# The state-space stage of a hybrid layer: the skip term D x made and added by GpSimd, finished chunks turned two chunks later, rows of u loaded by SyncE

## The chip, the cores and the metric

The kernel runs on one core of one Trainium2 chip. The metric is the device time of one execution in microseconds; the median of three runs stands for a kernel.

## What is computed

One layer of a network that mixes attention and a two-way state-space scan (Mamba-2 SSD), for 1024 latent and 256 context tokens, in 32-bit floats. The change lies in the state-space part alone. Of the reference, cut to that part:

```python
CHUNK = 128            # 10 chunks of 128 tokens: 8 latent, 2 of context
SSM_HEADS, SSM_HEAD_DIM, D_STATE = 8, 64, 128

def ssd_chunked(x, dt, a, bm, cm, init_state):
    ...
    lmat = jnp.exp(jnp.where(causal, seg, -jnp.inf))            # seg: differences of cumulated dt * a
    cb = jnp.einsum("bclgn,bcsgn->bgcls", cc, bc)
    y_diag = jnp.einsum("bgcls,bgrcls,bcsgrp->bclgrp", cb, lmat, xr)
    ...
    final, entering = lax.scan(step, init_state, (chunk_decay, chunk_states))
    y_off = jnp.einsum("bclgn,cbgrpn,bgrcl->bclgrp", cc, entering, jnp.exp(a_cs))
    y = (y_diag + y_off).reshape(b, l, h, p)
    return y, final.reshape(b, h, p, n)

def ssm_mixer(...):
    ...
    y_f, fin_f = ssd_chunked(xs, dt_f, a_f, bm, cm, init_f)
    y_b, fin_b = ssd_chunked(flip(xs), flip(dt_b), a_b, flip(bm), flip(cm), init_b)
    y = y_f + flip(y_b) + d_skip.astype(f32)[:, None] * xs.astype(f32)
    y = y.reshape(b, l, SSM_WIDTH) * jax.nn.silu(z.astype(f32))
    return rms_norm(y, g_out).astype(z.dtype), fin_f, fin_b
```

## The kernel before

The kernel is written engine by engine: each engine has its own list of instructions in an order set by hand, and semaphores between them. A wait stands in front of an instruction, and everything behind it on that engine waits too. `phase_front` holds the input projection, the gate z, a backward sweep over the chunks that makes the backward states, and then the loop over the ten chunks (`for c in range(NT)`) that this case is about. Before the loop TensorE turns x, token by feature, chunk after chunk (`turn_x`), and ScalarE copies it out of PSUM into `xs(c)`, a part of `chunks_hi`; the untransposed x stays in `xbcT`.

For one chunk c of the loop, PSUM banks are called A[0] to A[3] and Q (four banks):

- **TensorE** makes the two carried products into A[1] and A[2] (line 1431), then the exponents' differences of the chunk after, `segments(c + 1)`, into Q: four times a product of `up` with `pick` (line 1391) and one that adds the mask (line 1393). Rows 64 and 65 of `pick` hold this chunk's rows of u, loaded from DRAM. Then `contribution(c)` to the state (line 1368), `scores(c + 1)` (line 1414), and into A[3] the skip term as four products with a diagonal matrix `ddiag` (line 1443) and the in-chunk product with the weights `wt` (line 1448). Last it turns the finished rows of the chunk before, `y_turn(c - 1)`, into A[0] (line 1399).
- **VectorE** scales A[1] and A[2] by the decays (lines 1158 and 1160, the second into `off_b`), adds the two (line 1164), makes the next state (line 1150) and the weights of the next chunk (lines 1137 and 1140), then adds A[3] (line 1171) and multiplies by the gate (line 1172), which is `y_ready`.
- **ScalarE** squares the finished y with a sum (`square`, line 864, into `yn`), takes the exponential of Q (`exponents`, line 875) and copies the scores to `cb` (line 877), scales y to `yn` (`scale`, line 869), copies the turned rows from PSUM over the gate (`mix`, line 881, which is `mix_ready`), and weighs x for the next contribution (`weigh`, line 888, eight instructions).
- **GpSimd** decays the forward state (line 685), makes the reciprocal root of the mean square (`rstd`, lines 690 and 691), and issues the load of u for chunk c + 2 (line 697).
- **SyncE** waits for `mix_ready`, stores the chunk's mixed rows (line 627), waits for that store and loads attention's rows over them (`load_landed`, lines 388 to 390).

Q, A[0] and A[3] are single. `pick`, `yv`, `wt`, `xw` and the state `sf` have two slots each. In the code P is 128, NT is 10, NT_LAT is 8, NS is 9, and SW is 512.

Of the kernel before, what the change touches and what calls it, by code (L numbers as in the profile page):

```python
# [23 lines left out]
P = 128  # L24
F32 = mybir.dt.float32
# [10 lines left out]
NT = T // P  # L36
# [35 lines left out]
C_GPRE, C_GFFN, C_BMOD, C_GQ, C_GKV, C_CW, C_CB, C_GS, C_DB, C_AL, C_DS = 0, 8, 16, 64, 67, 69, 93, 101, 105, 121, 137  # L72
N_COLS = 141
# [319 lines left out]
def phase_front(L):  # L393
# [6 lines left out]
    with ExitStack() as st:  # L400
# [31 lines left out]
        ddiag = at("ddiag", "conv_acc", 2048, [P, 4, P])  # L432
# [31 lines left out]
        def turn_bank(n):  # L464
# [17 lines left out]
        u_loaded = [L.own_sem(f"ss_u{i}") for i in range(2)]  # L482
# [6 lines left out]
         rstd_ready, yn_ready, y_turned, mix_ready, sf_ready, dec_ready, fin_mm, fin_cp, consts, pch) = (  # L489
# [4 lines left out]
                 "sf_ready", "dec_ready", "fin_mm", "fin_cp", "consts", "pch"))  # L494
# [48 lines left out]
        dskip = L.cols[:, C_DS:C_DS + 4]  # L543
# [20 lines left out]
        def _(sp):  # L564
# [51 lines left out]
            sp.wait_ge(q_stored, 16)  # L616
            for c in range(NT):
# [7 lines left out]
                if c < NT - 1:  # L625
                    sp.wait_ge(mix_ready, c + 1)
                    sp.dma_start(quads(L.mixS[c]), zt(c)).then_inc(mix_stored, 16)

        @block.gpsimd
        def _(pool):  # L630
# [45 lines left out]
            p.link(pool.memset(nh[:], -0.5))  # L676

# [15 lines left out]
            def load_u(c):  # L693

                if c >= 2:
                    pool.wait_ge(seg_done, c - 1)
                pool.dma_start(pick[64:66, c % 2, :, :], L.u_s[:, :, chunk(c)]).then_inc(u_loaded[c % 2], 16)

            until(pool, tiles[-1])
            load_u(0)  # L700
            load_u(1)
# [11 lines left out]
        def _(act):  # L713
# [119 lines left out]
            def constants(i):  # L833
# [26 lines left out]
            def square(c):  # L860
                act.wait_ge(y_ready, c + 1)
                if c >= 1:
                    act.wait_ge(y_turned, c)
                act.activation(yn[:], yv[:, c % 2, :], ACT.Square, accum_out=ss[:, c:c + 1]).then_inc(squared, 1)

            def scale(c):
                act.wait_ge(rstd_ready, c + 1)
                act.wait_ge(squared, c + 1)
                act.activation(yn[:], yv[:, c % 2, :], ACT.Copy, scale=rs[:, c:c + 1]).then_inc(yn_ready, 1)
# [2547 lines left out]
```

## Time and profile before

| | |
|---|---|
| median of three runs | 1667.59 us (1666.72 to 1667.93) |
| the profiled execution | 1670.06 us, its span 1668.2 us |
| TensorE busy / VectorE / ScalarE / GpSimd, share of the span | 97% / 61% / 42% / 6% |
| the loop over chunks | from about 350 to 428 us of the span |
| granted TensorE clock, whole span | 0.994 of full |

The profile is of one execution. "PE" is TensorE's matmul, "DVE" VectorE, "ACT" ScalarE, "POOL" GpSimd, "SPq" the issue of a DMA by SyncE. Starts of neighbours on one engine can lie closer than the duration printed, since the end of one overlaps the start of the next; the distance from start to start is then what an instruction costs.

### The profile page before, as it was taken

The numbers are of one execution on the slowest core, as the hardware profiler recorded it, in microseconds if no ns is written. First come the engines' busy times: TensorE is split into PE (matmuls) and PEld (weight loads), VectorE is DVE, ScalarE is ACT, GpSimd is POOL, SyncE is SP. The second block draws the span as 40 slices with busy tenths as digits, with TensorE's granted clock in tenths as the row PEclk, the third lists the DMA queues.
The fourth block names the chain that finished last, engine by engine and source line by source line (L and its number), as shares of the span: only waits on it lengthen the run. The fifth ranks groups of instructions, "written<-read, shape, count | busy, mean of one in ns | idle before, by whom it ended". The sixth has DMA issues, their size and how long they took to land. (4 is left out here: it accounts for less than half of the span.)

```text
span 1668.2 us, 25023 instructions
## 1 busy us (share of the span) xinstructions
PE 1621.0 (97%) x9735; PEld 1414.1 (85%) x9735; DVE 1017.8 (61%) x1689; ACT 705.7 (42%) x1288; POOL 100.4 (6%) x123
## 2 busy tenths in 40 slices
PE   6999999999899999999999999999999999999997
PEld 4787878877688988878889999999999998888886
DVE  4653645268655555554587656666665665477788
ACT  4632112357554444545664333333333334434453
POOL 1101000013000000320000000000000000000011
PEclk9999999999999999999999999999999999999999
DMA  9324441013200000323312222212222226663445
GB/s 372 149 98 145 158 155 52 1 56 105 74 20 1 14 1 1 108 89 133 127 51 87 97 80 93 106 73 98 91 97 81 92 81 219 232 217 97 126 162 191
DMA packets 76294, 176.36 MB, mean 106 GB/s; under 512 B 10353, under 2 KB 26945, under 8 KB 74129
## 3 DMA queue, kind: packets, MB, share of 16 engines
q1 hardware_dynamic: 72080, 169.75, 29.3%
q0 software_dynamic: 4096, 5.01, 0.9%
q8 instruction: 79, 1.29, 0.3%
q14 instruction: 39, 0.31, 0.1%
HBM read 131.02 MB, written 43.70 MB: 105 GB/s over the span
## 5 line engine op out<-in xcount | busy, mean ns | idle before, releaser
L374 PE MATMUL psF<-gv,gu_ring 128*128 128x384 f32 (+1 forms) x664 | 220.6, 332 | 3.9 <-DVE gv L2748 3.2
L375 PE MATMUL psF<-gv,gu_ring 128*128 128x384 f32 (+1 forms) x664 | 220.1, 332 | 0.0
L376 PE MATMUL psF<-gv,gu_ring 128*128 128x384 f32 (+1 forms) x664 | 220.1, 331 | 0.0
L381 PE MATMUL psF<-gv,gu_ring 128*128 128x512 f32 x540 | 193.6, 392 | 0.0
L382 PE MATMUL psF<-gv,gu_ring 128*128 128x256 f32 x540 | 151.3, 280 | 0.0
L374 PE MATMUL psF<-d_w_ring,d_hid_ring 128*128 128x512 f32 x360 | 140.2, 389 | 0.0
L375 PE MATMUL psF<-d_w_ring,d_hid_ring 128*128 128x512 f32 x360 | 140.1, 389 | 0.0
L376 PE MATMUL psF<-d_w_ring,d_hid_ring 128*128 128x512 f32 x360 | 140.1, 389 | 0.0
L374 PEld LDWEIGHTS psF<-gv,gu_ring 128*128 128x128 f32 x664 | 125.3, 189 | 10.4 <-issue 3.6
L375 PEld LDWEIGHTS psF<-gv,gu_ring 128*128 128x128 f32 x664 | 125.5, 189 | 0.0
L374 PE MATMUL psP<-hT_hi,win_hi 128*128 128x512 f32 (+1 forms) x336 | 123.7, 368 | 1.8 <-DVEq L1085 1.5
L376 PEld LDWEIGHTS psF<-gv,gu_ring 128*128 128x128 f32 x664 | 125.3, 189 | 0.0
L376 PE MATMUL psP<-hT_hi,win_lo 128*128 128x512 f32 (+1 forms) x336 | 119.2, 355 | 0.0
L375 PE MATMUL psP<-hT_lo,win_hi 128*128 128x512 f32 (+1 forms) x336 | 119.1, 354 | 0.0
L2543 ACT ACTIVATE hraw<-psF 128x384 f32<-128x384 f32 (+1 forms) x130 | 56.8, 439 | 138.9 <-PE psF L376 84.2
L381 PEld LDWEIGHTS psF<-gv,gu_ring 128*128 128x128 f32 x540 | 101.1, 187 | 16.6
L382 PEld LDWEIGHTS psF<-gv,gu_ring 128*128 128x128 f32 x540 | 101.9, 189 | 0.0
L1846 DVE TENSOR_TENSOR pt_lo<-psPT,pt_hi 128x512 fp32r<-128x512 f32 (+1 forms) x104 | 58.9, 583 | 43.8 <-ACT pt_hi L1706 43.6
L2590 ACT ACTIVATE d_hid_ring<-d_hid 128x640 fp32r<-128x640 f32 x54 | 40.0, 740 | 98.4 <-PE psF L376 98.4
L374 PEld LDWEIGHTS psF<-d_w_ring,d_hid_ring 128*128 128x128 f32 x360 | 67.6, 188 | 14.6 <-DVE hraw L3007 0.5
L375 PEld LDWEIGHTS psF<-d_w_ring,d_hid_ring 128*128 128x128 f32 x360 | 67.6, 188 | 14.0
L376 PEld LDWEIGHTS psF<-d_w_ring,d_hid_ring 128*128 128x128 f32 x360 | 67.6, 188 | 13.9
(457 smaller groups left out, 3704.3 us busy)
## 6 DMA issues: line engine op xcount, KB each, us to landing
hid_variants<-hraw SPq DMA_DIRECT2D x77, 320.0 KB, 2.2
d_hid<-hid_variants SPq DMA_DIRECT2D x58, 320.0 KB, 3.0
m_wring<-in_w_mod SPq DMA_DIRECT2D x16, 1024.0 KB, 4.9
d_b<-in_w_down SPq DMA_DIRECT2D x44, 256.0 KB, 4.5
win_raw<-in_w_in SPq DMA_DIRECT2D x18, 512.0 KB, 5.7
w_mod_staged<-in_w_mod SPq DMA_DIRECT2D x16, 512.0 KB, 15.3
d_hid_more<-hid_variants SPq DMA_DIRECT2D x19, 320.0 KB, 3.2
raw_gu<-in_w_gate SPq DMA_DIRECT2D x11, 512.0 KB, 3.8
```

The lines of the kernel that those rows point to most:

```text
L374: pe.matmul(out, w_hi, x_hi, start=first, stop=False, skip_group_check=onto)
L375: pe.matmul(out, w_hi, x_lo, start=False, stop=False, skip_group_check=onto)
L376: return pe.matmul(out, w_lo, x_hi, start=False, stop=last, skip_group_check=onto)
L381: pe.matmul(both, w_hi, x_both, start=first, stop=False, skip_group_check=onto)
L382: return pe.matmul(main, w_lo, x_hi, start=False, stop=last, skip_group_check=onto)
L1846: dve.tensor_tensor(pt_lo[:, g[0]:g[-1] + 1, r:r + P], psPT[:, (g0 + i) % 2, 0:len(g), :], pt_hi[:, g[0]:g[-1] + 1, r:r + P].bitcast(F32), ...
L2543: act.activation(dst[:, chunk(c)], psA(n, c), ACT.Copy).then_inc(main_copied if paired_up(n, c) else copied[c], 1)
L2590: act.activation(ring_h(e, 0), hr[e % HR], ACT.Copy).then_inc(h_hi, 1)
```

## The change

The skip term leaves TensorE. GpSimd makes `xd(c)`, x times D in token order, for all ten chunks before the loop, over the x in `xbcT` that has been turned. In the loop it adds xd(c) to `off_b` and then `off_b` to `yv` (`carried`), which VectorE did in one instruction before; VectorE waits for `y_summed` ahead of its addition of A[3]. `ddiag` and its 40 products go, and the four ScalarE instructions that filled it.

ScalarE's `weigh(c + 1)` now follows its exponentials directly, then comes `mix` of chunk c - 2 (it was c - 1), and `scale(c - 1)` last. TensorE's `y_turn` is of chunk c - 2 in pass c. The squares go to a tile of their own.

The rows of u of chunks 0 and 1 are loaded by GpSimd as before. The others are loaded by SyncE: chunks 2 and 3 ahead of its loop, chunk c + 4 at the end of its pass c.

```diff
+        sq_junk = at("y_sq_junk", "conv_acc", 2048, [P, SW])
+        dskip = at("d_skip", "conv_acc", 4608, [P, SH])[:]
...
+        xd = lambda c: L.xbcT[:, 0:4, chunk(c)]
@@ block.sync
+            def load_u(c):
+                sp.wait_ge(seg_done, c - 1)
+                sp.dma_start(pick[64:66, c % 2, :, :].bitcast(F32), L.u_s[:, :, chunk(c)]).then_inc(u_later[c % 2], 16)
+
+            load_u(2)
+            load_u(3)
             for c in range(NT):
                 if c >= 1:
                     sp.wait_ge(mix_stored, 16 * c)
                     load_landed(L, sp, in_hi, c - 1)
...
                 if c < NT - 1:
                     sp.wait_ge(mix_ready, c + 1)
                     sp.dma_start(quads(L.mixS[c]), zt(c)).then_inc(mix_stored, 16)
+                if c + 4 < NT:
+                    load_u(c + 4)
@@ block.gpsimd
+            pool.wait_ge(kr_stored, 32)
+            for i, c in enumerate(down):
+                pool.wait_ge(x_copied, 2 * i + 1)
+                p.mark(pool.tensor_tensor(heads4(xd(c)), heads4(xs(c)), per_head(dskip), ALU.mult))
+            p.wait()
+
+            def carried(c):
+
+                pool.wait_ge(off_b_read, c + 1)
+                p.link(pool.tensor_tensor(quads(off_b[:]), quads(off_b[:]), xd(c), ALU.add))
+                pool.wait_ge(off_f_read, c + 1)
+                pool.tensor_tensor(yv[:, c % 2, :], yv[:, c % 2, :], off_b[:], ALU.add).then_inc(y_summed, 1)
 
             pool.wait_ge(s_ready, NS)
             for c in range(NT):
                 decay(c)
+                carried(c)
                 if c >= 1:
                     rstd(c - 1)
-                if c + 2 < NT:
-                    load_u(c + 2)
@@ block.scalar
                     exponents(c + 1)
+                    weigh(c + 1)
+                if c >= 2:
+                    mix(c - 2)
                 if c >= 1:
                     scale(c - 1)
-                    mix(c - 1)
-                if c + 1 < NT:
-                    weigh(c + 1)
+            mix(NT - 2)
@@ block.vector
-                dve.wait_ge(off_f_read, c + 1)
-                dve.wait_ge(off_b_read, c + 1)
-                f.link(dve.tensor_tensor(yv[:, c % 2, :], yv[:, c % 2, :], off_b[:], ALU.add))
-
                 if c + 1 < NT:
                     next_state(c)
                     weights_in_chunk(c + 1)
 
+                dve.wait_ge(y_summed, c + 1)
                 dve.wait_ge(diag_done, c + 1)
@@ block.tensor
-                pe.wait_ge(u_loaded[c % 2], 16 * (c // 2 + 1))
+                if c < 2:
+                    pe.wait_ge(u_loaded[c], 16)
+                else:
+                    pe.wait_ge(u_later[c % 2], 16 * (c // 2))
...
-                for a in range(4):
-                    pe.matmul(A[3][:, chunk(a)], L.xbcT[:, a, chunk(c)], ddiag[:, a, :], start=(a == 0), stop=False)
...
-                if c >= 1:
-                    if c + 1 < NT:
-                        pe.wait_ge(cb_read, c + 2)
-                    if c >= 2:
-                        pe.wait_ge(mix_ready, c - 1)
-                    y_turn(c - 1)
+                if 2 <= c < NT - 1:
+                    pe.wait_ge(cb_read, c + 2)
+                    if c >= 3:
+                        pe.wait_ge(mix_ready, c - 2)
+                    y_turn(c - 2)
+            pe.wait_ge(mix_ready, NT - 2)
+            y_turn(NT - 2)
```

What stands on ScalarE in one pass of the loop, before. `seg` is the exponential, `cb` the copy of the scores, `yn<-yv,y_rs` the scaling, `chunks_hi<-psP` the mix, `xw` the weighing, and `yn,y_ss<-yv` the square:

```order
L875 ACTIVATE seg<-psP 128x2048 [waits ss_seg_done,ss_w_ready]
L877 ACTIVATE cb<-psP 128x256 [waits ss_cb_done]
L869 ACTIVATE yn<-yv,y_rs 128x512 [waits ss_squared,ss_rstd]
L881 ACTIVATE chunks_hi<-psP 128x4x128 [waits ss_y_turned]
L888 ACTIVATE xw<-chunks_hi,dt_feats 128x64 [waits ss_s_mm]
L888 ACTIVATE xw<-chunks_hi,dt_feats 128x64 x7
L864 ACTIVATE yn,y_ss<-yv 128x512 [waits ss_y_turned,ss_y_ready]
```

And now:

```order
L891 ACTIVATE seg<-psP 128x2048 [waits ss_seg_done,ss_w_ready]
L893 ACTIVATE cb<-psP 128x256 [waits ss_cb_done]
L904 ACTIVATE xw<-chunks_hi,dt_feats 128x64 [waits ss_s_mm]
L904 ACTIVATE xw<-chunks_hi,dt_feats 128x64 x7
L897 ACTIVATE chunks_hi<-psP 128x4x128 [waits ss_y_turned]
L885 ACTIVATE yn<-yv,y_rs 128x512 [waits ss_y_turned,ss_squared,ss_rstd]
L878 ACTIVATE y_sq_junk,y_ss<-yv 128x512 [waits ss_squared,ss_y_ready]
```

The weighing moved ahead of the mix and the scaling behind it; the exponential and the mix of one pass now have the eight weighing instructions between them.

What stands on SyncE in one pass of its loop, before (`ssm_mix_scratch` takes the mixed rows, the three loads behind it are attention's):

```order
L627 DMA ssm_mix_scratch<-chunks_hi 512x1x128 [waits ss_mix_ready]
L388 DMA chunks_hi<-q_scratch 128x3x128 [waits ss_mix_stored]
L389 DMA chunks_hi<-kv_scratch 128x2x128
L390 DMA chunks_hi<-kr_scratch 128x128
L627 DMA ssm_mix_scratch<-chunks_hi 512x1x128 [waits ss_mix_ready]
```

And now:

```order
L635 DMA ssm_mix_scratch<-chunks_hi 512x1x128 [waits ss_mix_ready]
L621 DMA pick<-u_scratch 2x16x128 [waits ss_seg_done]
L388 DMA chunks_hi<-q_scratch 128x3x128 [waits ss_mix_stored]
L389 DMA chunks_hi<-kv_scratch 128x2x128
L390 DMA chunks_hi<-kr_scratch 128x128
```

The load of u came between the store of a chunk and the wait for that store, so behind the wait for `mix_ready`.

What stands on TensorE now from one contribution to the next segments (`m_psC` is A[3], `m_psM` is A[2], `psP` holds Q, A[0] and A[1]):

```order
L1382 MATMUL psP<-xw,chunks_lo 128x256 [waits ss_xwf_ready,ss_off_f_read]
L1382 MATMUL psP<-xw,chunks_lo 128x256
L1431 MATMUL psP<-xbcT 128x128 [waits ss_mix_ready,ss_cb_read]
L1431 MATMUL psP<-xbcT 128x128
L1467 MATMUL m_psC<-chunks_hi,wt 32x64 [waits ss_w_ready,ss_y_ready]
L1467 MATMUL m_psC<-chunks_hi,wt 32x64 x31
L1416 MATMUL psP<-const,yn 128x128 [waits ss_yn_ready,ss_mix_ready,ss_cb_read]
L1416 MATMUL psP<-const,yn 128x128 x3
L1448 MATMUL psP<-sf,xbcT 128x256 [waits ss_off_b_read,ss_sf_ready]
L1448 MATMUL psP<-sf,xbcT 128x256
L1448 MATMUL m_psM<-chunks_lo,xbcT 128x256 x2
L1408 MATMUL psP<-pick,up_49 128x512 [waits ss_u_later1,ss_exp_done]
```

The four products with `ddiag` that stood ahead of the in-chunk product are gone, and the first product of the segments waits for SyncE's load instead of GpSimd's.

## Rows read from the trace of the kernel before

**Rows 1.** Timeline of TensorE, one pass: start us, us, engine, line, tiles

```profile
365.45 1.03 PE L1431 MATMUL psP<-sf,xbcT 128*128 128x256 f32 x4
...
367.00 0.58 PE L1391 MATMUL psP<-pick,up 66*128 66x512 f32 x1
...
369.02 1.03 PE L1368 MATMUL psP<-xw,chunks_lo 128*128 128x256 f32 x4
...
370.33 1.06 PE L1443 MATMUL m_psC<-ddiag,xbcT 128*128 128x128 f32 x8
371.32 1.10 PE L1448 MATMUL m_psC<-chunks_hi,wt 128*32 128x64 f32 x64
...
372.84 1.03 PE L1431 MATMUL psP<-sf,xbcT 128*128 128x256 f32 x4
```

**Rows 2.** Timeline of VectorE, the same pass; idle before it in brackets

```profile
368.13 0.68 DVE L1160 TENSOR_TENSOR off_b<-m_psM,dt_feats 128x512 f32<-128x512 f32 x1
368.92 0.70 DVE L1164 TENSOR_TENSOR yv<-yv,off_b 128x512 f32<-128x512 f32 x1
370.14 0.69 DVE L1150 TENSOR_TENSOR sf<-decayed,psP 128x512 f32<-128x512 f32 x1 [0.52 <-PE psP L1368]
371.19 1.23 DVE L1137 TENSOR_TENSOR wt<-seg 128x1024 f32<-128x1024 f32 x1 [0.36 <-ACT seg L875]
...
374.31 0.69 DVE L1172 TENSOR_TENSOR yv<-yv,chunks_hi 128x512 f32<-128x512 f32 x1
```

**Rows 3.** Timeline of ScalarE, the same pass

```profile
369.28 1.88 ACT L875 ACTIVATE seg<-psP 128x2048 f32<-128x2048 f32 x1 [0.51 <-PE psP L1393]
...
371.32 0.72 ACT L869 ACTIVATE yn<-yv,y_rs 128x512 f32<-128x512 f32 x1
373.04 0.60 ACT L881 ACTIVATE chunks_hi<-psP 128x512 f32<-128x512 f32 x1 [0.99 <-PE psP L1399]
373.53 2.01 ACT L888 ACTIVATE xw<-chunks_hi,dt_feats 128x64 f32<-128x64 f32 x8
375.44 0.62 ACT L864 ACTIVATE yn<-yv 128x512 f32<-128x512 f32 x1
```

**Rows 4.** Timeline of SyncE, the same pass: one issue

```profile
373.66 0.52 SPq L627 DMA_DIRECT2D ssm_mix_scratch<-chunks_hi  x1
```

**Rows 5.** DMA issues, the loop and the whole run: median us to landing last

```profile
ssm_mix_scratch<-chunks_hi SPq DMA_DIRECT2D x10, 256.0 KB, 2.6
...
chunks_hi<-kr_scratch SPq DMA_DIRECT2D x9, 64.0 KB, 2.7
...
pick<-u_scratch POOLq DMA_DIRECT2D x8, 16.0 KB, 2.9
...
cond<-in_cond SPq DMA_DIRECT2D x1, 8.0 KB, 1.7
```

**Rows 6.** Timelines of GpSimd and VectorE, and GpSimd's groups by form

```profile
350.48 1.04 POOL L685 TENSOR_TENSOR decayed<-sf,dt_feats 128x512 f32<-128x512 f32 x1 [66.00 <-DVEq L1129]
...
367.77 1.03 POOL L685 TENSOR_TENSOR decayed<-sf,dt_feats 128x512 f32<-128x512 f32 x1 [4.15 <-DVE yv L1172]
...
350.64 1.96 DVE L1137 TENSOR_TENSOR wt<-seg 128x1024 f32<-128x1024 f32 x1 [0.30 <-ACT seg L875]
...
L1789 POOL TENSOR_TENSOR wv_lo<-wv_raw,wv_hi 128x512 fp32r<-128x512 f32 x1 | 1.3, 1283 | 0.0
```

**Rows 7.** Timeline of ScalarE, the last passes

```profile
413.82 1.88 ACT L875 ACTIVATE seg<-psP 128x2048 f32<-128x2048 f32 x1 [0.74 <-PE psP L1393]
...
421.98 0.72 ACT L869 ACTIVATE yn<-yv,y_rs 128x512 f32<-128x512 f32 x1 [1.29 <-POOL y_rs L691]
...
427.19 0.60 ACT L881 ACTIVATE chunks_hi<-psP 128x512 f32<-128x512 f32 x1 [0.81 <-PE psP L1399]
```

**Rows 8.** TensorE behind the loop: timeline, and a window with the granted clock

```profile
431.13 0.77 PE L374 MATMUL psScore<-qn_hi,wq_hi 128*128 128x512 f32 x1 [3.97 <-DVE qn_lo L1854]
...
430.00:432.00 2.00, 0.87 (x2) 0.81 (x3) 2.00 (x4) 2.00 (x3) 0.00 (x0) 0.50 1.04 292
```

More of the change, by code:

```diff
@@ L481, in phase_front @@
             "kv_stored", "kr_stored", "q_stored", "cache_stored", "out_stored"))
-        u_loaded = [L.own_sem(f"ss_u{i}") for i in range(2)]
+        u_loaded, u_later = ([s(f"ss_{n}{i}") for i in range(2)] for n, s in (("u", L.own_sem), ("u_later", L.sem)))
         mix_stored, fin_out = (L.own_sem("ss_" + n) for n in ("mix_stored", "fin_out"))
@@ L691, in rstd @@
                 pool.tensor_tensor(rs[:, c:c + 1], ms[:, c:c + 1], nh[:], ALU.pow).then_inc(rstd_ready, 1)
-            def load_u(c):
-                if c >= 2:
-                    pool.wait_ge(seg_done, c - 1)
-                pool.dma_start(pick[64:66, c % 2, :, :], L.u_s[:, :, chunk(c)]).then_inc(u_loaded[c % 2], 16)
             until(pool, tiles[-1])
-            load_u(0)
-            load_u(1)
+            for c in range(2):
+                pool.dma_start(pick[64:66, c, :, :], L.u_s[:, :, chunk(c)]).then_inc(u_loaded[c], 16)
+            pool.wait_ge(kr_stored, 32)
[8 more added lines that the diff above has]
+                pool.tensor_tensor(yv[:, c % 2, :], yv[:, c % 2, :], off_b[:], ALU.add).then_inc(y_summed, 1)
             pool.wait_ge(s_ready, NS)
@@ L846, in constants @@
                                    ).then_inc(ones_set, 1)
-                elif i == 6:
-                    for a in range(4):
-                        act.activation(ddiag[:, a, :], L.ident, ACT.Copy, scale=dskip[:, a:a + 1]).then_inc(consts, 1)
             act.wait_ge(conv_read, N_XBC)
@@ L868, in scale @@
                 act.wait_ge(squared, c + 1)
+                if c >= 1:
+                    act.wait_ge(y_turned, c)
                 act.activation(yn[:], yv[:, c % 2, :], ACT.Copy, scale=rs[:, c:c + 1]).then_inc(yn_ready, 1)
@@ L986, in take_u @@
                 dve.wait_ge(u_turned, n + 1)
-                dst = (u2, L.up2)[which]
+                dst = (u2.bitcast(F32R), L.up2)[which]
                 dve.tensor_copy(dst[0:64, c * P:(c + 2) * P], (psD, psE)[n % 2][0:64, :]).then_inc(u_read, 1)
@@ L1410, in scores @@
                     pe.wait_ge(cb_read, c)
-                if c >= 3:
-                    pe.wait_ge(mix_ready, c - 2)
+                if c >= 4:
+                    pe.wait_ge(mix_ready, c - 3)
                 for g in range(2):
@@ L1433, in _ @@
                 mm.then_inc(off_done, 1)
+                if c == NT - 1:
+                    pe.wait_ge(cb_read, NT)
+                    pe.wait_ge(mix_ready, NT - 3)
+                    y_turn(NT - 3)
                 if c + 1 < NT:
@@ L1448, in _ @@
                         mm = pe.matmul(A[3][rows, h * SP_:(h + 1) * SP_], wt[:, c % 2, h, rows],
-                                       xs(c)[:, h // 2, (h % 2) * SP_:(h % 2 + 1) * SP_], start=False, stop=(h == SH - 1))
+                                       xs(c)[:, h // 2, (h % 2) * SP_:(h % 2 + 1) * SP_], start=(h == 0), stop=(h == SH - 1))
                 mm.then_inc(diag_done, 1)
-                if c >= 1:
-                    if c + 1 < NT:
-                        pe.wait_ge(cb_read, c + 2)
-                    if c >= 2:
-                        pe.wait_ge(mix_ready, c - 1)
-                    y_turn(c - 1)
+                if 2 <= c < NT - 1:
[5 more added lines that the diff above has]
+            y_turn(NT - 2)
             pe.wait_ge(off_f_read, NT)
@@ L3398 @@
             col(a["g_ssm_out"][0]), np.tile(a["dt_bias"].reshape(1, 16), (P, 1)),
-            np.tile(a["a_log"].reshape(1, 16), (P, 1)),
-            np.repeat(a["d_skip"][0].reshape(4, 2).T, P // 2, axis=0)], axis=1),
-        "b_mod": a["b_mod"], "g_post_mix": a["g_post_mix"], "g_post_ffn": a["g_post_ffn"],
+            np.tile(a["a_log"].reshape(1, 16), (P, 1))], axis=1),
+        "d_skip": a["d_skip"], "b_mod": a["b_mod"], "g_post_mix": a["g_post_mix"], "g_post_ffn": a["g_post_ffn"],
         "w_mod": w_mod.reshape(KD, P, MOD_ALL, MOD_W).transpose(2, 1, 0, 3).reshape(MOD_ALL, P, KD * MOD_W), "w_in": np.stack([k_tiles(in_tile(*e)) for e in TILES] + z_tiles),
```

18 lines of the change are left out of this document (8 added, 10 removed).

## The prediction, made before the changed kernel ran

> **What bounds the kernel now.** I read the windows first: TensorE is the only engine without gaps in the loop over chunks. Its timeline over one pass then shows what a pass is made of [rows 1]: the carried product starts at 365.45 and again at 372.84, so a pass takes 7.39 us, and no row in it has idle time before it. The four products with `ddiag` run from 370.33 to 371.32, 0.99 us of it. VectorE's and ScalarE's timelines [rows 2, 3] show the opposite: idle times of 0.3 to 1.0 us, each ended by TensorE or by the exponential. So the loop runs at TensorE's pace, and what the change takes off TensorE could be won, if no chain through the other engines is longer than the 6.40 us that remain. I therefore followed each chain that returns to itself after one pass, by the order of instructions and their waits, with durations from the rows.
>
> **What the change removes.** TensorE loses 0.99 us in each pass. VectorE loses the addition at 368.92, 0.79 us from the start of `off_b`'s row to its own with the wait, and 0.70 for itself [rows 2]. ScalarE loses the four copies into `ddiag` before the loop, which ran beside TensorE's products: nothing. GpSimd's DMA issue leaves the loop; nobody waits for GpSimd there.
>
> **What it adds to GpSimd.** Ten products before the loop, each like `decayed` (1.03 us, one operand repeated over a head [rows 6]), one per z tile of TensorE, which takes several us: hidden, but for the last. That one reads when VectorE starts the last weighing of the sweep; I count up to 0.3 us. In the loop two additions of two full operands. No row shows that form at 128x512 but `wv_lo`, 1.28 us [rows 6]; the other bound is `decayed`, 1.03. I take 1.28, as both its operands are full. 0.16 us to see the semaphore, two additions and a gap of 0.09 make 2.8 us behind `off_b`. VectorE needs the sum only ahead of A[3]: in the steady loop it is there in time.
>
> **What it moves, the load of u.** This is the term that decides. SyncE loads u of chunk c + 4 behind the store of chunk c, and the store waits for `mix` of chunk c. ScalarE does `mix(c)` in pass c + 2, after exp(c + 3) and the eight weighings. TensorE needs that u for segments(c + 4), one pass later, exp(c + 4) needs the segments, and `mix(c + 1)` stands behind exp(c + 4). So one pass now contains:
>
> - exp to mix: exp to the instruction behind `cb` is 371.32 - 369.28 = 2.04, the weighing 375.44 - 373.53 = 1.91 [rows 3]: 3.95 us. TensorE turns the chunk meanwhile (it waits only for `cb` of this pass), so it does not delay the mix.
> - the mix itself, 0.60 [rows 3]; SyncE's store issue begins 0.02 later (373.64 to 373.66) and takes 0.52 [rows 4], with 0.04 to the next issue: 0.56.
> - the load of u, from issue to landing, L.
> - 0.1 to wake TensorE, then segments to exp: 367.00 to 369.28 = 2.28 [rows 1, 3].
>
> Sum: 3.95 + 0.60 + 0.02 + 0.56 + L + 0.10 + 2.28 = 7.51 + L. Even with L = 0 that is over 7.39. For L the trace has no 16 KB load by SyncE in the loop. Bounds: 1.7 (8 KB by SyncE, queue empty, `cond`) and 2.9 (the same rows by GpSimd, whose issue itself is in it); the store just ahead on the same queue takes 2.6 and the small load behind two others 2.7 [rows 5]. I take 2.4, since it follows a 256 KB store by 0.56 and is small. A pass is then 9.91 us (9.2 to 10.4). Whatever else was near TensorE's pace is hidden under it: TensorE stands still 2.5 to 3.5 us a pass ahead of the segments.
>
> The Trainium skill ("DMA: Bandwidth & Descriptors", Anatomy of one DMA) puts the fixed cost of one DMA at about 2.0 us whatever its size; by that, as an estimate, a pass would be 9.5 us and the time 1683.4. The rows of the loop are above it.
>
> Chunks 2 and 3 are loaded early, so the chain governs from exp(3) to exp(9), six passes. Before, these stood at 369.28 and 413.82 [rows 3, 7], 44.54 us. Now 6 x 9.91 = 59.46: **+14.9** (+10.7 to +17.9).
>
> **Start.** Passes 0 to 2 run without that chain. The one that is left goes from y ready over `off_b` (368.81, 1.20 behind the y ready that GpSimd answers at 367.77 with 0.16 delay), the two additions, the weights and the next y. While GpSimd reads SBUF, a VectorE instruction with two SBUF operands seems to be held: at 350.64 the first `wt<-seg` took 1.96 us where the others take 1.23, and `decayed` ran on GpSimd from 350.48 to 351.52 [rows 2, 6]. So a pass costs 1.20 + 0.16 + 1.28 + 0.09 + 1.28 - 0.15 (the hold ends before the row) + 3.81 (371.19 to 375.00, `wt` to y ready [rows 2]) = 7.67, or about 7.5 when VectorE gets in first; without the hold it is exp to y ready, 1.91 + 3.81, and the square before exp, 0.76: 6.48. I take **+0.6** up to exp(3) (-1 to +1.5).
>
> That hold is a rule of the Trainium skill ("SBUF — State Buffer", Who interferes with whom): a VectorE instruction with two SBUF inputs and a GpSimd instruction that reads SBUF block each other, whoever starts second waits for the whole of the other. The trace agrees, by the 1.96 us. It speaks against the change: by it the additions give back more than VectorE saves.
>
> **End.** Behind exp(9), y(8) is ready after 5.7 us as before. Then the last chunk has nothing beside it: VectorE waits for both additions (2.9 us in place of 0.79), and GpSimd's root for chunk 8 stands behind them, so `scale(8)` starts some 10.7 us after exp(9), where it was 421.98 - 413.82 = 8.2 [rows 7]. From there the turns and the last mix take what they took (427.19 - 421.98 = 5.2 [rows 7]), a little more. **+2.7** (+1 to +4).
>
> **Sum.** 14.9 + 0.6 + 2.7 = +18.2 us. The profiled execution took 1670.06 us with a span of 1668.2; it would take 1688.3. The median of the runs is 2.5 lower, 1667.59, so I forecast 1685.8. The rest of the kernel has no reason to move: attention begins when the last rows are mixed.
>
> **Rivals.**
>
> 1. *The clock falls as well.* Behind the loop TensorE idles 3.97 us, and its first product then takes 0.77 us at a granted clock of 0.50, that is 1.2 instead of 2.4 GHz [rows 8]. The new idle time of about 2.7 us in each pass is shorter, and the loop is 65% busy; gaps of 1.1 us in the old loop did nothing. Were the clock low in part of the loop, segments (2.28) and the turn ahead of the mix would stretch by 1.5 to 3 us a pass: +8 to +15 more, about 1697.
> 2. *The load of u is hidden anyway* (lands before TensorE is there), and the hold on the SBUF port governs: 7.5 to 7.7 a pass, 9 x 0.2 + 2.7 = +4.5, 1672. Against it: the order puts the load behind the mix without exception.
> 3. *Faster: TensorE's saving comes through.* A pass of 6.5, no hold and no wait for u: 9 x -0.9 + 2.7 = -5.4, 1662. It decides only if the way from mix to mix is under 7.39; it is 7.51 plus the transfer.
> 4. *The change does what it says and the stage is hidden behind something else*: no; the loop stands alone between projection and attention, and nothing of the other stages lies beside it.
>
> **How the numbers follow.** The forecast has 82 in 100, the clock 10, the hidden load 5, the faster case 3. The transfer's bounds with start and end give +12 to +24 for the forecast, 1680 to 1692. Reaching toward the clock case and the skill's figure I say 1678 to 1694. Less than 0.2% (3.3 us) cannot be told from no change here. Slower by more: 95; within: 2; faster: 3.
>
> **What the profile of the changed kernel would show.** Exponentials about 9.9 us apart from exp(3) on; TensorE idle ahead of the first product of `pick`, put down to the DMA into `pick`; each SyncE load of u 0.56 us behind a store, and that 0.02 behind a mix. No `ddiag`. Four or five `wt<-seg` at 1.23 again, as GpSimd is done by then, and one or two longer ones in passes 0 to 2. GpSimd's additions at 1.03 or 1.28. I am wrong if the exponentials lie 6.5 to 7.7 us apart (rivals 2, 3), if TensorE's idle time is put down to another, or if the granted clock in the loop is under 1 (rival 1).

## The result, and the profile after it

The changed kernel takes 1699.92 us (median of four runs, 1698.69 to 1703.93); the kernel before took 1667.68 in the same job (1666.72 to 1667.93). The ratio is 1.019, with a 95% interval of 1.0177 to 1.0203: 32 us slower. The forecast was 1685.8 us, with a range of 1678 to 1694. The sign is right and the size is not: the change costs 32 us where I had 18.

The profiled execution took 1700.36 us with a span of 1698.4 and a mean granted clock of 0.984 (0.994 before). The busy times of the whole run hardly differ (TensorE 96%, VectorE 60%, ScalarE 41%, GpSimd 8%), so the time lies in the loop. ScalarE's timeline has the exponentials (`seg`) and the mixes (`chunks_hi<-psP`), from exp(3) on:

```profile
369.50 1.86 ACT L891 ACTIVATE seg<-psP 128x2048 f32<-128x2048 f32 x1
...
380.97 1.88 ACT L891 ACTIVATE seg<-psP 128x2048 f32<-128x2048 f32 x1 [3.74 <-PE psP L1410]
384.92 0.58 ACT L897 ACTIVATE chunks_hi<-psP 128x512 f32<-128x512 f32 x1
392.95 1.88 ACT L891 ACTIVATE seg<-psP 128x2048 f32<-128x2048 f32 x1 [5.35 <-PE psP L1410]
...
440.74 1.88 ACT L891 ACTIVATE seg<-psP 128x2048 f32<-128x2048 f32 x1 [4.99 <-PE psP L1410]
```

From exp(3) to exp(9) it takes 71.24 us, 11.87 a pass, where before it took 44.54 [rows 3, 7]. ScalarE's idle time before the exponential was 0.51 and is now 3.7 to 5.4, ended by TensorE's segments. What TensorE waited for, and how long the segments took, is in SyncE's timeline and TensorE's, of the same pass:

```profile
385.52 0.56 SPq L635 DMA_DIRECT2D ssm_mix_scratch<-chunks_hi  x1
386.13 0.62 SPq L621 DMA_DIRECT2D pick<-u_scratch  x1
```

```profile
389.00 0.77 PE L1408 MATMUL psP<-pick,up 66*128 66x512 f32 x1 [3.11 <-DMA pick<-u_scratch]
...
389.66 0.98 PE L1408 MATMUL psP<-pick,up 66*128 66x512 f32 x1
...
392.64 1.92 PE L1382 MATMUL psP<-xw,chunks_lo 128*128 128x256 f32 x4
```

The chain of the prediction stands there link by link: exponential to mix 3.95 us (380.97 to 384.92), mix to the store's issue 0.60, store to load 0.61, the load's issue to TensorE's first product 2.87, and from there to the next exponential 3.95 (389.00 to 392.95); together 11.98. Four links are as forecast or nearly. The last is not: it was 2.28 [rows 1, 3]. A product with `pick` takes 0.98 instead of 0.58, the contribution 1.92 instead of 1.03 [rows 1]. Those are the durations at the clock's lower level, 1.2 GHz. In every second pass the last link is 3.5, and the low clock reaches the first one as well: `cb` waits 0.55 for the scores, so that exponential to mix takes 4.61 (392.95 to 397.56). The windows of the loop, 10 us each, give the granted clock in the third column from the end (2.4 GHz is 1.00):

```profile
364.00:374.00 10.00, 8.77 (x139) 6.71 (x128) 9.06 (x9) 7.81 (x23) 8.42 (x7) 1.00 0.01 2
374.00:384.00 10.00, 6.96 (x88) 4.46 (x87) 5.32 (x7) 4.49 (x11) 5.85 (x6) 0.83 0.24 67
384.00:394.00 10.00, 6.89 (x22) 4.14 (x21) 3.97 (x6) 3.89 (x10) 4.31 (x5) 0.71 0.24 69
...
434.00:444.00 10.00, 7.21 (x80) 4.77 (x80) 3.56 (x6) 3.49 (x8) 4.32 (x5) 0.66 0.38 108
```

The clock is at full speed until exp(3) and low for part of every pass after it. The waits add up to one cause (us in total, times, longest):

```profile
PE psP L1408 <- DMA pick<-u_scratch: 17.8, 6, 3.1
```

Behind exp(9) the loop's end is longer too. VectorE's and ScalarE's timelines of the last chunk:

```profile
451.01 0.69 DVE L1185 TENSOR_TENSOR yv<-yv,m_psC 128x512 f32<-128x512 f32 x1 [2.71 <-POOL yv L719]
451.73 0.69 DVE L1186 TENSOR_TENSOR yv<-yv,chunks_hi 128x512 f32<-128x512 f32 x1
```

```profile
451.91 0.72 ACT L885 ACTIVATE yn<-yv,y_rs 128x512 f32<-128x512 f32 x1 [3.58 <-POOL y_rs L702]
453.57 0.60 ACT L897 ACTIVATE chunks_hi<-psP 128x512 f32<-128x512 f32 x1 [0.93 <-PE psP L1416]
454.06 0.62 ACT L878 ACTIVATE y_sq_junk<-yv 128x512 f32<-128x512 f32 x1
...
458.94 0.60 ACT L897 ACTIVATE chunks_hi<-psP 128x512 f32<-128x512 f32 x1 [2.50 <-PE psP L1416]
```

TensorE's timeline of the same stretch, the turn of chunk 8, the contribution behind it, and the turn of chunk 9:

```profile
452.78 0.75 PE L1416 MATMUL psP<-const,yn 128*128 128x128 f32 x4 [4.44 <-ACT yn L885]
453.32 1.92 PE L1382 MATMUL psP<-xw,chunks_lo 128*128 128x256 f32 x4
...
457.84 1.06 PE L1416 MATMUL psP<-const,yn 128*128 128x128 f32 x4
```

From exp(9) to the end of the last mix it takes 18.80 us (440.74 to 459.54), where it took 13.97 [rows 7]: +4.8. Start, loop and end make 0.2 + 26.7 + 4.8 = +31.7. The first product of attention now starts at 462.40, where it started at 431.13 [rows 8], +31.3, and the profiled executions differ by 30.3. So the loss lies wholly in this stage, and about 1 us of it is given back later.

### The profile page after: what moved, and what is told of

The parts are those of the page before. It is cut to its first block and busy times, and to the rows that moved or that the text cites. A ratio compares the mean times of both kernels' runs of the same rounds, so it can differ in the third digit from the quotient of the medians.

```text
span 1698.4 us, 24899 instructions
## 1 busy us (share of the span) xinstructions
PE 1627.6 (96%) x9655; PEld 1413.0 (83%) x9655; DVE 1020.1 (60%) x1679; ACT 704.6 (41%) x1284; POOL 133.4 (8%) x146
## 3 DMA queue, kind: packets, MB, share of 16 engines
q8 instruction: 78, 1.28, 0.3%
```

## The experiments

Ten kernels were run. The kernel before ran beside each of them, with medians of 1668.75 to 1669.71 us, so ratios are given with each; where times of different jobs are subtracted, the result is good to 1 to 2 us.

### u_gpsimd: the changed kernel, u loaded by GpSimd again

```diff
@@ gpsimd, loop, behind rstd(c - 1)
+                if c + 2 < NT:
+                    pool.wait_ge(seg_done, c + 1)
+                    pool.dma_start(pick[64:66, c % 2, :, :], L.u_s[:, :, chunk(c + 2)]).then_inc(u_more[c % 2], 16)
@@ sync: no load_u
```

> The changed kernel with one part undone: GpSimd loads all rows of u, chunk c + 2 in its pass c, as before. If the wait for u behind the mix costs the time, and the fallen TensorE clock hangs on that wait: exponentials 7.5 to 7.8 us apart (the hold between GpSimd's additions and wt<-seg governs), no row of TensorE idle for pick, granted clock 1.00 in the loop, time about 1672 (1669 to 1676). If GpSimd's additions or the later mix were the main cost, the time stays over 1690. If nothing else than u is lost and the hold costs nothing: 1662.

Measured: 1694.58 us (1694.21 to 1694.81), ratio 1.0155 (1.014 to 1.017). A clear miss. Giving the load back to its old engine does not bring the old time back, because that engine's queue is no longer what it was. GpSimd's timeline and TensorE's:

```profile
384.02 1.27 POOL L711 TENSOR_TENSOR yv<-yv,off_b 128x512 f32<-128x512 f32 x1
...
385.38 1.04 POOL L693 TENSOR_SCALAR y_ms<-y_ss 128x1 f32<-128x1 f32 x1
386.51 1.55 POOL L694 TENSOR_TENSOR y_rs<-y_ms,y_nh 128x1 f32<-128x1 f32 x1
388.02 0.68 POOL L721 DMA_DIRECT2D pick<-u_scratch  x1
```

```profile
390.91 0.77 PE L1400 MATMUL psP<-pick,up 66*128 66x512 f32 x1 [3.95 <-DMA pick<-u_scratch]
...
391.57 0.98 PE L1400 MATMUL psP<-pick,up 66*128 66x512 f32 x1
```

The load stands behind both additions and the root of the chunk, and is issued 5.83 us behind its exponential (382.19). TensorE waits up to 4.1 us for it, about every second pass: the exponentials lie 12.1 to 12.7 and 6.5 to 7.7 us apart in turn. The wait for u is the same fault by another queue, and the clock is low here too (0.76 to 0.93 in the windows from 374 to 444).

### u_early: the load ahead of the wait for the mix

```diff
@@ sync, loop
+                if c + 4 < NT:
+                    load_u(c + 4)
                 if c < NT - 1:
                     sp.wait_ge(mix_ready, c + 1)
                     sp.dma_start(quads(L.mixS[c]), zt(c)).then_inc(mix_stored, 16)
-                if c + 4 < NT:
-                    load_u(c + 4)
```

> The changed kernel with SyncE's load of u of chunk c + 4 put ahead of its wait for the mix of chunk c instead of behind the store, so one pass earlier. Theory (the place in SyncE's order, not the engine): the same as with GpSimd's loads, within 1 us, about 1672. Rival (a SyncE load as such, or its queue, is late): TensorE still idle for pick, over 1680.

Measured: 1674.25 us (1672.55 to 1676.87, six runs), ratio 1.0034 (1.0022 to 1.0045), clock 0.995 in the profiled execution. Moving two lines gives back about 26 of the 32 us. No wait for `pick` is left. A pass now takes 7.61 us, the way that rival 2 had worked out (7.67), and all engines' rows of one pass show what sets it:

```profile
377.46 1.86 ACT L891 ACTIVATE seg<-psP 128x2048 f32<-128x2048 f32 x1
...
379.47 1.27 POOL L719 TENSOR_TENSOR yv<-yv,off_b 128x512 f32<-128x512 f32 x1
379.56 2.27 DVE L1154 TENSOR_TENSOR wt<-seg 128x1024 f32<-128x1024 f32 x1 [0.21 <-DVE sf L1167]
380.82 1.05 POOL L701 TENSOR_SCALAR y_ms<-y_ss 128x1 f32<-128x1 f32 x1
```

`wt<-seg` takes 1.23 us alone [rows 2] and 2.27 beside GpSimd's second addition, which had started 0.09 earlier and had 1.18 us left. Then it is GpSimd that is held: `y_ms`, one element in each partition, takes 1.05 where it takes 0.19 alone.

### no_adds: u_early without GpSimd's additions in the loop

```diff
@@ carried(c), gpsimd
-                pool.wait_ge(off_b_read, c + 1)
-                p.link(pool.tensor_tensor(quads(off_b[:]), quads(off_b[:]), xd(c), ALU.add))
-                pool.wait_ge(off_f_read, c + 1)
-                pool.tensor_tensor(yv[:, c % 2, :], yv[:, c % 2, :], off_b[:], ALU.add).then_inc(y_summed, 1)
@@ vector
-                dve.wait_ge(y_summed, c + 1)
+                dve.wait_ge(off_f_read, c + 1)
```

This kernel leaves the skip term and the backward carried part out of y; no engine adds them.

> u_early with GpSimd's two additions in the loop left out and not done elsewhere (the backward carried part and D times x are missing from y). What they cost apart from u. Theory (a VectorE instruction with two SBUF operands is held while GpSimd reads SBUF): wt<-seg at 1.23 instead of about 2.3, a pass of 6.4 to 6.6 us, time 1657 to 1661, some 12 less than u_early. Rival (GpSimd's additions run beside everything): the same time as u_early within 1 us.

Measured: 1666.52 us (1665.28 to 1669.05, ten runs), ratio 0.9989 (0.9979 to 0.9998), 0.45% under u_early. `wt<-seg` is back at 1.23 and the free passes take 6.54 to 6.56 us, close to the 6.48 worked out for a loop without the hold. So GpSimd's two additions, the hold and the wait for them in the last chunk together, cost u_early 0.45%, about 7.5 us; how much of it is the hold alone this kernel does not separate. It gained less than the 12 us expected. The other passes take 6.7 to 7.9 us; in the longest of them TensorE waits 1.01 us for `pick`. And a part is lost behind the loop: the last mix ends 10.9 us earlier than in u_early (423.03 against 433.96), but attention's first product starts only 7.2 us earlier (429.70 against 436.92), for a reason that lag_only shows below. Even with the additions left out, the kernel is only 0.1% under the one before.

```profile
361.38 1.87 ACT L888 ACTIVATE seg<-psP 128x2048 f32<-128x2048 f32 x1
...
363.45 1.23 DVE L1151 TENSOR_TENSOR wt<-seg 128x1024 f32<-128x1024 f32 x1 [0.21 <-ACT seg L888]
...
367.92 1.86 ACT L888 ACTIVATE seg<-psP 128x2048 f32<-128x2048 f32 x1
```

```profile
429.70 0.76 PE L374 MATMUL psScore<-qn_hi,wq_hi 128*128 128x512 f32 x1 [7.31 <-DVE qn_lo L1871]
```

### one_add: one addition on GpSimd, the other on VectorE

```diff
@@ carried(c), gpsimd
-                p.link(pool.tensor_tensor(quads(off_b[:]), quads(off_b[:]), xd(c), ALU.add))
-                pool.wait_ge(off_f_read, c + 1)
-                pool.tensor_tensor(yv[:, c % 2, :], yv[:, c % 2, :], off_b[:], ALU.add).then_inc(y_summed, 1)
+                pool.tensor_tensor(quads(off_b[:]), quads(off_b[:]), xd(c), ALU.add).then_inc(y_summed, 1)
@@ vector, ahead of the addition of A[3]
                 dve.wait_ge(y_summed, c + 1)
+                dve.wait_ge(off_f_read, c + 1)
+                f.link(dve.tensor_tensor(yv[:, c % 2, :], yv[:, c % 2, :], off_b[:], ALU.add))
```

(Over u_early.)

> u_early with the second addition (off_b to yv) back on VectorE, just ahead of that of A[3]; GpSimd adds only D times x to off_b, which ends before wt<-seg starts. Nothing is left out. Theory (the hold acts when GpSimd reads SBUF during wt<-seg): wt<-seg back at 1.23, a pass 7.61 - 1.04 + 0.72 = about 7.3 us, time 1667 to 1669. Rival (the longer wt<-seg has another cause): wt<-seg stays at 2.3, a pass over 8, slower than u_early by over 4 us.

Measured: 1672.04 us (1670.06 to 1673.62, ten runs), ratio 1.0022 (1.0013 to 1.0031). The pass is 7.26 us as expected, and the hold is gone:

```profile
378.22 1.28 POOL L717 TENSOR_TENSOR off_b<-off_b,xbcT 128x512 f32<-128x512 f32 x1
...
379.66 1.23 DVE L1152 TENSOR_TENSOR wt<-seg 128x1024 f32<-128x1024 f32 x1 [0.21 <-ACT seg L889]
```

GpSimd's addition ends at 379.50, 0.16 ahead of `wt<-seg`. VectorE has 0.7 us more work in a pass and is still 0.35 us faster. But the end, from exp(9) to the last mix, takes 18.43 us and not 13.97 (it was 18.46 in u_early), and that 4.5 us takes the loop's gain and more. The expectation of 1667 to 1669 had left it out.

### lag_only: the new order of ScalarE and the later turns alone, over the kernel before

```diff
@@ scalar, loop (the skip term, VectorE's addition and GpSimd's loads as before)
                     exponents(c + 1)
+                    weigh(c + 1)
+                if c >= 2:
+                    mix(c - 2)
                 if c >= 1:
                     scale(c - 1)
-                    mix(c - 1)
-                if c + 1 < NT:
-                    weigh(c + 1)
+            mix(NT - 2)
@@ tensor: y_turn(c - 2) as in the change
```

> The kernel before with ScalarE's new order and the turns of chunk c - 2 alone (the squares go to a free tile); D times x on TensorE, u loaded by GpSimd. Theory: TensorE still makes the pass, 7.39 us apart, its last passes take up to 1 us more; 1667 to 1669. Rival (the later mix itself costs time, for instance at the start of attention): over 1671.

Measured: 1670.83 us (1668.97 to 1672.02, ten runs), ratio 1.0011 (1.0002 to 1.002): within 0.2% of before. The pass is 7.39 us and the end 13.96, both those of before, so the later turns cost nothing in the loop. Behind it they do. SyncE's timeline and TensorE's:

```profile
422.37 0.52 SPq L627 DMA_DIRECT2D ssm_mix_scratch<-chunks_hi  x1
...
426.57 0.52 SPq L627 DMA_DIRECT2D ssm_mix_scratch<-chunks_hi  x1
...
433.84 0.76 PE L374 MATMUL psScore<-qn_hi,wq_hi 128*128 128x512 f32 x1 [6.72 <-DVE qn_lo L1862]
```

The later mixes leave the stores of chunks 7, 8 and 9 to the end, and SyncE waits for each store before it goes on. The store of chunk 8 is issued at 426.57, 2.50 us behind its mix (before: at 424.14, right behind it), the last at 431.25 (before: 428.53). Attention's first product starts at 433.84, 2.7 us later than before [rows 8], though the last mix ends at the same time (427.75 against 427.79). The measured 0.11% is about 1.8 us. In the changed kernel this is hidden: its last mix is so late that attention starts only 2.86 us behind its end (462.40 against 459.54).

### u_alone: SyncE's loads of u alone, over the kernel before

```diff
@@ sync
+            load_u(2)
             for c in range(NT):
...
                     sp.wait_ge(mix_ready, c + 1)
                     sp.dma_start(quads(L.mixS[c]), zt(c)).then_inc(mix_stored, 16)
+                if c + 3 < NT:
+                    load_u(c + 3)
@@ gpsimd
-                if c + 2 < NT:
-                    load_u(c + 2)
```

> The kernel before with one part alone: rows of u from chunk 2 on loaded by SyncE, chunk 2 ahead of its loop, chunk c + 3 behind the store of chunk c. D times x stays on TensorE, the mix of chunk c - 1 and the weighing in their old order. Theory (a load behind the mix makes the pass, whatever else is changed): exp to mix 3.76, then 0.60, 0.58, 2.8 and 2.25 as in fill10, so exponentials 9.9 to 10.2 apart from exp(2) or exp(3) on, six or seven passes times 2.6: about 1685 at the full clock. TensorE is busy 7.39 us of a pass here and idle some 2.5; if that idle time lowers the clock as in the changed kernel, about 1697. Rival (the place in SyncE's order does harm only together with the turns two chunks later): under 1672.

Measured: 1695.29 us (1693.95 to 1699.07), ratio 1.0166 (1.0152 to 1.018). This part alone makes some 27 us (1.66%), with every addition where it was. It also shows the clock at work. TensorE's timeline, the first product of the segments in two passes that follow each other and in a later one, then the windows around them:

```profile
379.77 0.93 PE L1400 MATMUL psP<-pick,up 66*128 66x512 f32 x2 [2.19 <-DMA pick<-u_scratch]
...
389.68 1.52 PE L1400 MATMUL psP<-pick,up 66*128 66x512 f32 x2 [2.29 <-DMA pick<-u_scratch]
...
391.09 0.98 PE L1400 MATMUL psP<-pick,up 66*128 66x512 f32 x1
...
414.67 0.93 PE L1400 MATMUL psP<-pick,up 66*128 66x512 f32 x2 [2.59 <-DMA pick<-u_scratch]
```

```profile
375.00:385.00 10.00, 7.80 (x119) 5.95 (x108) 6.49 (x9) 5.88 (x14) 2.10 (x3) 1.00 0.24 67
385.00:395.00 10.00, 7.71 (x32) 4.90 (x26) 4.49 (x7) 4.61 (x12) 2.09 (x3) 0.74 0.24 70
...
415.00:425.00 10.00, 7.79 (x101) 6.02 (x102) 6.31 (x8) 5.87 (x14) 1.08 (x2) 1.00 0.24 68
```

Behind a gap of 2.19 us the clock held and the pass took 9.8 us; behind the next, 2.29, it fell and the pass took 11.6. Between 415 and 425 it is at full speed, behind a gap of 2.59, the longest of all. So with gaps like these it falls in some passes only, and the length of the gap just before does not tell in which.

### fill10 and fill4: TensorE kept busy while it waits for u

```diff
@@ segments(c), tensor, ahead of the wait for u (the change otherwise as it is)
                 else:
+                    if c >= 4:
+                        for k in range(10):        # fill4: range(4)
+                            pe.matmul(Q[:, k % 4, :], identb[:], flat(maskb[:, 0, :, :]), start=True, stop=True)
                     pe.wait_ge(u_later[c % 2], 16 * (c // 2))
```

The products go to Q, which the segments then overwrite; they add work and take none away.

> The changed kernel, with ten 128x512 bf16 products (about 0.22 us each at the full clock) on TensorE ahead of its wait for u from chunk 4 on; their results are overwritten. Theory (the idle time lowers the clock, which stretches segments): the clock stays at 1.00, the transfer is still waited for, a pass costs 9.9 to 10.3 us, time 1686 to 1690. Rival (the clock has another cause, or the load of TensorE is not what counts): time unchanged at 1700, or later by up to 6 x 2 us.

Measured: 1688.43 us (1686.94 to 1690.2), ratio 1.0119 (1.0101 to 1.0136). Sixty more products make the kernel 11.5 us faster. TensorE's timeline:

```profile
385.07 2.32 PE L1406 MATMUL psP<-maskb,identb 128*128 128x512 bf16 x10
388.61 0.50 PE L1411 MATMUL psP<-pick,up 66*128 66x512 f32 x1 [1.21 <-DMA pick<-u_scratch]
...
388.99 0.59 PE L1411 MATMUL psP<-pick,up 66*128 66x512 f32 x1
```

TensorE still waits for the same load, but for 1.21 us instead of 3.11; the clock is 1.00 in all windows from 374 to 434, and a pass takes 10.1 us. The links of one pass: 3.94 from the exponential (380.65) to the mix (384.59), 0.61 and 0.61 to the load's issue (385.81), 2.80 to TensorE (388.61), 2.23 to the next exponential (390.84). The chain is untouched and only its last link has come back to full speed.

> The changed kernel with four instead of ten filler products of TensorE ahead of the wait for u in each pass from chunk 4 on. They leave about 1.9 to 2.4 us of idle TensorE in a pass instead of 2.8 to 3.1. If the clock holds at such a gap: 1687 to 1690 us, as with ten. If it falls at it, as it did in some passes of u_alone at 2.2 to 2.3 us: up to 1700, as the changed kernel.

Measured: 1695.53 us (1689.63 to 1696.68, four runs), ratio 1.0148 (1.0132 to 1.0164). Both outcomes that were named occurred, in different executions. The profiled one took 1689.63 us with a mean clock of 0.994, a pass of 10.0 to 10.2 us and gaps of up to 2.5:

```profile
388.69 0.50 PE L1411 MATMUL psP<-pick,up 66*128 66x512 f32 x1 [2.50 <-DMA pick<-u_scratch]
```

The other three took 1694.78 to 1696.68 us with mean clocks of 0.985 to 0.991. They have no timeline, so in which passes the clock fell there is not shown. The same instructions, with the same chain, thus cost 5 to 7 us more or less by the clock alone.

### fill10_u_first: fill10, and the load ahead of the store instead of behind it

```diff
@@ sync, loop, over fill10
                     sp.wait_ge(mix_ready, c + 1)
+                    if c + 4 < NT:
+                        load_u(c + 4)
                     sp.dma_start(quads(L.mixS[c]), zt(c)).then_inc(mix_stored, 16)
-                if c + 4 < NT:
-                    load_u(c + 4)
```

> fill10 with the load of u ahead of the store instead of behind it (both behind the wait for the mix). Theory (the sum mix, store issue, load, segments is a chain): a pass loses the store's issue, 0.6 us, 6 passes: 3 to 4 us less than fill10, about 1685; if the store's transfer also delays the load's landing, 2.8 becomes less and it is more than that. Rival (the load's place behind the store is hidden): as fill10.

Measured: 1685.18 us (1683.36 to 1686.06), ratio 1.01 (1.0084 to 1.0115), 3.3 us under fill10. A pass takes 9.3 us instead of 10.1: 0.61 of it is the store's issue, and about 0.15 the load itself, which has no 256 KB ahead of it on the queue (from its issue to TensorE's product it takes 2.44 to 2.73, mean 2.57, against 2.64 to 2.80, mean 2.72, in fill10). The link that is taken out of the chain shortens the pass by its own length, as a chain must.

### tuned: the best version that the experiments pointed to

```diff
@@ over one_add: sync loads u of chunk c + 5 behind the store of chunk c; and
@@ scalar
                 act.activation(flat(seg[:]), flat(Q[:]), ACT.Exp).then_inc(exp_done, 1)
+                if c >= 2:
+                    square(c - 2)
@@ vector and gpsimd: both additions of the last chunk are VectorE's
+                if c == NT - 1:
+                    f.link(dve.tensor_tensor(quads(off_b[:]), quads(off_b[:]), xd(c), ALU.add))
```

> The version in which GpSimd adds only the D product to off_b, with SyncE loading u of chunk c+5 behind the store of chunk c, the last chunk's two additions done by VectorE, and ScalarE's square(c-1) behind its exponential instead of ahead of it. Theory: the loop's loads have a whole pass of slack, so a pass takes about 7.05 us (7.26 less the square's wait ahead of the exponential), and the end about +0.7 us over before instead of the +4.5 of one_add, since no GpSimd addition and no turn held for it stands in the last chunk: 1665 to 1667 us, 0.1 to 0.2% below before. Rival: the order of the square does nothing and the end stays long for its turns of two chunks before: about 1670 to 1672, as one_add.

Measured: 1672.53 us (1669.57 to 1673.78, eleven runs), ratio 1.0015 (1.0006 to 1.0024). It does not beat the kernel before; the rival came true. Most passes stay at 7.25 to 7.28 us (two take 7.6), as the exponential now waits 1.1 us for the segments: the square was not in its way. VectorE's timeline shows the ring that sets it:

```profile
389.69 0.68 DVE L1177 TENSOR_TENSOR yv<-psP,dt_feats 128x512 f32<-128x512 f32 x1
...
391.60 0.69 DVE L1169 TENSOR_TENSOR sf<-decayed,psP 128x512 f32<-128x512 f32 x1 [0.63 <-PE psP L1391]
392.50 1.23 DVE L1156 TENSOR_TENSOR wt<-seg 128x1024 f32<-128x1024 f32 x1 [0.21 <-DVE sf L1169]
...
396.35 0.69 DVE L1195 TENSOR_TENSOR yv<-yv,chunks_hi 128x512 f32<-128x512 f32 x1
396.95 0.68 DVE L1177 TENSOR_TENSOR yv<-psP,dt_feats 128x512 f32<-128x512 f32 x1
```

TensorE's contribution waits until VectorE has read A[1] (L1177), `sf` waits for the contribution, and everything else on VectorE stands behind `sf`; it has 0.84 us idle in a pass, all in these two waits. The end is 18.0 us long (412.16 to 430.16) without any addition of GpSimd in the last chunk. So the +4 us at the end do not need GpSimd's additions there, as I had believed. The trace shows where they lie: y(8) is ready 1.24 us later behind its exponential, as VectorE now adds `off_b` itself and stands behind the ring; GpSimd's root of chunk 8 is 0.65 later, as `y_ms` and `y_rs` run beside VectorE's two additions of the last chunk (0.70 and 1.00 us); and TensorE, idle 2.80 us ahead of the turn of chunk 8, does what follows at the lower clock, which costs another 2.1.

## Why the prediction was right about the sign and wrong about the size

**The chain through the load of u.** Right, and shown from three sides: the timeline has it link by link; u_early, which takes the load out of it, gets about 26 us back; u_alone, which has only that, loses 27. The forecast of a pass, 9.91, is met at full clock by fill10's 10.1. The 0.2 between them is L: 2.4 and 0.1 to wake TensorE were set, 2.64 to 2.80, mean 2.72, measured (fill10), inside the bounds of 1.7 and 2.9. The decision between the bounds leaned to the middle because the load is small; the row that stood nearest, the same 16 KB rows at 2.9 by another queue [rows 5], would have been better. The Trainium skill ("DMA: Bandwidth & Descriptors", Anatomy of one DMA) puts the fixed cost of a DMA at about 2.0 us, and gives this for DMAs that GpSimd issues, which the prediction left out when it used it for SyncE's. The loads of u that TensorE waited for took longer on either queue: 2.44 (fill10_u_first) to 3.06 (u_alone) by SyncE and 2.59 to 3.11 by GpSimd (u_gpsimd), from issue to TensorE's product.

**The clock: the step that failed.** It is rival 1, which had 10 in 100. The prediction said that the new idle time "is shorter" than the 3.97 us behind the loop, that "the loop is 65% busy" and that "gaps of 1.1 us in the old loop did nothing". That was an interpolation between two rows, 1.1 without effect and 3.97 with it, and the new gap of 2.7 was put on the harmless side of it with no row to say so. The new gap measured 2.8 to 3.1 us, and the clock was low for part of each pass. What that costs is at least the difference between the changed kernel and fill10, 1699.92 less 1688.43 = 11.5 us, in the middle of the +8 to +15 that rival 1 had worked out. In the traces 10.6 of it lies between exp(3) and exp(9) (71.24 against 60.63) and 1.6 in the end (18.8 against 17.2), with 1.0 taken back at the start. With both open, the range should have reached past rival 1's 1697. (The bounds of the terms themselves add up to +10.7 to +23.4, not to the +12 to +24 that the prediction gives; that changes nothing here.)

**With the clock held up in the loop** the forecast was 2.6 us low (1688.43 against 1685.8). By terms: the loop 1.2 (60.63 against 59.46, L); the end 0.5 (17.2 - 13.97 = +3.2 against +2.7; in it 2.4 for the additions and 0.9 for turns at the lower clock, which fell behind the loop in fill10 too, 0.53 in the window from 442 to 444); the start 0.6 (fill10's exp(3) at 370.46, +1.2 against +0.6; in the changed kernel itself it is +0.2). The 2.5 us by which I went from the profiled execution to the median was worth little: the median of three was at the low end of what the kernel before gave in later jobs.

**The start and the hold.** Right. While nothing waited for u, `wt<-seg` took 2.26 to 2.33 us in passes 0 to 2 and 1.23 in the six later ones (four or five short ones and one or two long ones were forecast):

```profile
371.62 2.27 DVE L1154 TENSOR_TENSOR wt<-seg 128x1024 f32<-128x1024 f32 x1 [0.21 <-DVE sf L1167]
```

The pass that the prediction worked out for a loop under the hold, 7.67, is 7.61 in u_early, and 6.48 without it is 6.56 in no_adds. The additions took 1.26 to 1.28 us, the value taken and not 1.03. Here the rule of the Trainium skill ("SBUF — State Buffer", Who interferes with whom), that whoever starts second waits for the whole of the other, was the better guide than the engines' work: one_add gives VectorE an instruction more, and its pass is 0.35 us shorter. The trace agrees nearly: `wt<-seg` was prolonged by 1.04 when 1.18 of GpSimd's addition was left.

**The end.** +4.8 against +2.7. The first half was right: VectorE waits 2.71 us for the additions, and `scale(8)` starts 11.17 us behind exp(9), where 10.7 was forecast and 8.16 was before. Of these 3.0 us the additions make 2.4, as fill10 shows with 10.53; the other 0.6 is a later y(8), behind a contribution of 1.92 us at the lower clock.

What failed is the other half, "from there the turns and the last mix take what they took (5.2), a little more": from `scale(8)` to the last mix it takes 7.03 us (451.91 to 458.94). Nearly all of the difference, 1.7, lies between `scale(9)` and the last mix (455.71 to 458.94 is 3.23, where it was 1.53). The turn of chunk 9 stands behind the contribution and the turns of the final state, which run at the lower level of the clock (0.50 in the window from 454 to 464): it starts 2.13 us behind `scale(9)` instead of 0.87, and takes 1.06 instead of 0.63. So of the +4.8 the clock makes about 2.5, and a mechanism that the prediction had only as rival 1, for the loop, acts behind the loop as well.

The traces say when it does. TensorE's idle time ahead of the turn of chunk 8, for a y that is late, then the duration of the contribution behind it and of the turn of chunk 9, and the length of the end, all in us:

| kernel | idle | contribution | turn of chunk 9 | end |
|---|---|---|---|---|
| before | 1.06 | 1.03 | 0.63 | 13.97 |
| lag_only | 1.06 | 1.03 | 0.63 | 13.96 |
| no_adds | 1.77 | 1.03 | 0.63 | 13.66 |
| tuned | 2.80 | 1.91 | 1.06 | 18.00 |
| one_add | 3.69 | 1.92 | 1.06 | 18.43 |
| u_early | 4.07 | 1.91 | 0.60 | 18.46 |
| u_gpsimd | 4.36 | 1.60 | 1.06 | 18.42 |
| changed kernel | 4.44 | 1.92 | 1.06 | 18.80 |
| fill10 | 4.46 | 1.92 | 0.60 | 17.20 |

Where y is not late, the clock stays up here. No run filled this gap as fill10 filled the others, so that the gap brings the clock down is read from the comparison and not tested by itself.

**The rivals.** Rival 1 came true. Rivals 2 and 3 are not what this change does, but both of their times were right for the kernels in which they hold: 1672 for the hidden load (u_early 1674.25), 6.5 us a pass for the free loop (no_adds).

## What to carry to other kernels

Before an instruction is moved to another engine's queue, write down what stands ahead of it there and what that waits for. Here a 16 KB load stood behind a wait for `mix`, which stood behind the exponential that needed the load four chunks on, and 2.8 us of latency became part of every pass. Moving it ahead of that one wait, two lines, removes four fifths of the loss.

A new gap on TensorE in every pass of a loop can be charged twice: once for its length and once for the clock. If no row shows what the clock does at gaps of that length, both cases belong in the range; and a kernel with filler products ahead of the wait tells the two costs apart.

Look also at the end of the stage. An order that costs nothing in the steady loop (lag_only) pushed three stores, each waited for, behind it, and attention started 2.7 us late.

Work given to an idle GpSimd is not free if it reads SBUF at the time when VectorE reads two SBUF operands: look where on VectorE's timeline it will fall, not at how much room the engine has.

## What the runs showed of the hardware

- Gaps of TensorE of 2.2 to 3.1 us, one in each pass of 10 to 12 us, can bring its clock to 1.2 GHz, and do so irregularly. In u_alone gaps of 2.40, 2.19, 2.59 and 2.21 left it at 2.4 GHz, and others of 2.29, 2.21 and 2.44 were followed by rows at half speed; fill4, with gaps of up to 2.5, held 0.994 over one whole execution and had 0.985 to 0.991 in three others. With gaps of at most 1.21 (fill10) it never fell in the profiled loop. Behind the loop, one gap of 2.80 (tuned) to 4.46 us (fill10) was followed by the lower level in each of eight traces, one of 1.06 to 1.78 in none of four (before, lag_only, no_adds, u_alone).
- The hold between VectorE and GpSimd reaches GpSimd's smallest instructions. `y_ms` and `y_rs` of one element per partition take 0.19 and 0.55 us alone, 1.05 and 1.53 beside `wt`. A queue with a few small instructions in it is thus up to 1.8 us longer than its rows show when alone, which is part of why u_gpsimd failed.
- The load of u, 16 KB, takes 2.63 to 3.06 us on SyncE's queue behind a 256 KB store (changed kernel, fill10, fill4, u_alone), from its issue to the product of TensorE that waits for it, and 2.44 to 2.73 ahead of the store (fill10_u_first). The profile gives no landing time for these loads.
